# Normalising expert outputs group by group inside the expert stage, with the scatter-adds of a step no longer waiting for one another

## The chip, the cores and the metric

One core of one Trainium2 chip runs the whole program. The metric is device time in microseconds, the median of three runs. The engines are TensorE (PE in the rows; PEld is its weight load), VectorE (DVE), ScalarE (ACT), GpSimd (POOL) and SyncE (SP), whose queue issues plain transfers; GpSimd issues the indirect ones (gather and scatter by a list of row numbers).

## What is computed

One layer over 4096 tokens of width 1024, in float32: a Fourier mixer, a layer norm, a mixture of experts, and a second layer norm.

```
y = fourier_mixer(x, w_in, w_out)
x = layer_norm(ALPHA * x + y, ln_g[0], ln_b[0])
scores = sigmoid(x @ w_router)                 # 32 experts in 4 groups of 8
group = argmax(sum of the two best (scores + b_router) of each group)
expert_idx = the two best experts inside that group
y = sum over the two experts of gate * (silu(x @ w_gate[e]) * (x @ w_up[e])) @ w_down[e]
x = layer_norm(ALPHA * x + y, ln_g[1], ln_b[1])
```

Both experts of a token lie in one group, so a token's sum is complete once the eight experts of its group are done. With the reference's inputs its routing gives the four groups 992, 1017, 1033 and 1054 tokens, and the experts, in order: 243, 248, 228, 257, 289, 307, 203, 209, 278, 289, 220, 242, 258, 266, 246, 235, 249, 265, 273, 272, 298, 202, 199, 308, 251, 239, 206, 278, 281, 245, 257 and 351.

## The kernel before

The first part (the Fourier mixer, the first norm and the router, in `GROUPS` = 16 steps) stores each normalised row twice: in `hd` ("h_rows"), from which the experts read, and in `acc` ("sums"), to which they add. GpSimd's `list_tokens` scatters (token, gate) entries into one list per expert. The lists are first filled with padding entries that point to spare rows behind the 4096 tokens.

The expert stage runs over *units* of up to `UNIT` = 320 tokens of one expert. A table `utab` gives a unit's expert and its row in the lists. An expert with at most 320 tokens is one unit; the last has two, so there are 33. A unit with at most `NARROW` = 256 tokens is *narrow* (17 of them), the others *wide* (16); a wide unit has a third, half-size token tile "c" beside "a" and "b". Each engine runs its own loop over units, tied to the others by semaphores:

- SyncE loads a unit's twelve weight pieces (`wraw`, six slots) and the entries of a coming unit (`load_entries`).
- ScalarE and VectorE split each piece in a high and a low part (`split`: cast on ScalarE, subtraction on VectorE), since each product is made of three passes.
- TensorE does the gate products (four blocks `k`), the up products (four blocks `k`, two PSUM banks, so that block 2 waits until VectorE has read block 0), the transposes of the next unit's rows, and then the down products.
- VectorE multiplies gate and up (`hid`), ScalarE casts it (`hidT` high part), VectorE makes the low part. The down product needs all four.
- GpSimd scatter-adds the results `yrow_a`, `yrow_b` (and `yrow_c`) to `acc` and gathers rows for the unit after next (`xrow`).

In the unit of GpSimd the scatter-add of tile b waits for that of tile a to land. These lines are before's:

```
for t in range(2):
    ...
    if t:
        own_wait(pool, y_out, 32 * u + 16, pool_gate)
    scatter(t, P, y_out)
```

After the last unit a tail loads the 32 tiles of `acc` in row order, normalises each (VectorE statistics and gain, ScalarE root and scaling, GpSimd the addition of `ln_b`) and stores it.

## Time and profile before

| | |
|---|---|
| median of 3 runs | 2350.23 us (2346.81 to 2350.3) |
| profiled execution, its own time | 2350.37 us |
| its span in the trace | 2348.4 us |
| TensorE busy | 2127.3 us, 91% |
| VectorE, ScalarE, GpSimd busy | 58%, 43%, 25% |
| first part, until the first unit's matmuls | 0 to 860.6 us |
| units | 860.6 to about 2211 us |
| tail, after the last scatter-add has landed | 2219.0 to 2348.4 us |

An engine's busy share is an average over these three parts, so what a change is worth is read in the part where it acts. Times in rows are microseconds from the span's start unless marked ns.

### The profile page before, as it was taken

The page shows a single profiled execution, that of the slowest core. Times are in us where ns is not written, and L with a number is a line of the kernel's source. Part 1 is how long each engine was busy: PE and PEld are TensorE (multiplying, and loading weights), DVE is VectorE, ACT ScalarE, POOL GpSimd, SP SyncE. Part 2 cuts the span into 40 slices and gives each one's busy share as a digit, 9 for nine tenths or more (in the row PEclk, how much of TensorE's full clock was granted, in tenths as well). Part 3 has the DMA queues.
Part 4 walks back from the last instruction along what each step waited for, and adds up shares of the span by engine and source line. Part 5 has one row for each costly group of instructions (what it writes and reads, how often), then busy time and mean ns, then how long its engine had stood idle before and what let it go on. Part 6 is the DMA issues. An engine that isn't in the chain of part 4 may idle for free.

```text
span 2348.4 us, 37687 instructions
## 1 busy us (share of the span) xinstructions
PE 2127.3 (91%) x12222; PEld 1801.6 (77%) x12223; DVE 1373.1 (58%) x2254; ACT 998.2 (43%) x1442; POOL 582.7 (25%) x493
## 2 busy tenths in 40 slices
PE   8999899999999449999999999999999999999600
PEld 3443678888888349999999999999999999998500
DVE  3321148888887746555655656555555565555298
ACT  1221123333233226555555645655455565554143
POOL 1000034444544411211121121212111121211166
PEclk9999999999999769999999999999999999999855
DMA  6880233443333347767776866877677777766376
GB/s 226 283 287 21 67 126 113 147 147 125 116 127 108 126 153 210 222 203 195 219 216 184 248 194 211 227 223 197 180 220 218 219 218 228 209 202 183 98 286 238
DMA packets 136067, 435.59 MB, mean 185 GB/s; under 512 B 30912, under 2 KB 35008, under 8 KB 131904
## 3 DMA queue, kind: packets, MB, share of 16 engines
q1 hardware_dynamic: 98592, 307.12, 38.6%
q0 software_dynamic: 37440, 128.01, 21.6%
q8 instruction: 21, 0.34, 0.1%
q14 instruction: 14, 0.11, 0.0%
HBM read 328.01 MB, written 108.10 MB: 186 GB/s over the span
## 4 chain that ended last, share of the span: by engine, by line
PE 90%; POOL 3%; issue 3%; DMA 2%; DVE 2%; ACT 0%; SPq 0%; POOLq 0%; ACTq 0%; DVEq 0%
PE ps L877 36%; PE ps L901 15%; PE ps L759 15%; PE ps L696 5%; POOL fin_r L1689 3%; PE ps L865 3%; PE ps L741 3%; PE ps L909 2%; PE ps L715 2%; PE ps L793 2%; PE ps L650 1%; PE ps L780 1%; PE ps L700 1%; PE ps L870 1%; PE ps L659 1%
## 5 line engine op out<-in xcount | busy, mean ns | idle before, releaser
L901 PE MATMUL ps<-wd_hi,hidT 128*128 128x512 f32 x1056 | 293.0, 402 | 0.4 <-ACT hidT L1099 0.4
L1359 DVE TENSOR_TENSOR wd_lo<-wraw,wd_hi 128x1024 fp32r<-128x1024 f32 x132 | 161.9, 1226 | 199.0 <-ACT wd_hi L1057 198.7
L901 PEld LDWEIGHTS ps<-wd_hi,hidT 128*128 128x128 f32 x1056 | 190.1, 189 | 36.3 <-ACT hidT L1099 0.8
L1359 DVE TENSOR_TENSOR wg_lo<-wraw,wg_hi 128x1024 fp32r<-128x1024 f32 x132 | 161.4, 1224 | 92.6 <-ACT wg_hi L1057 92.5
L1632 POOL DMA_INDIRECT sums<-yrow_a,ent_now x33 | 57.2, 1733 | 558.4 <-DVE yrow_a L1422 515.4
L1359 DVE TENSOR_TENSOR wu_lo<-wraw,wu_hi 128x1024 fp32r<-128x1024 f32 x132 | 160.7, 1218 | 52.0 <-ACT wu_hi L1057 51.9
L877 PE MATMUL ps<-mxT_hi,wg_hi 128*128 128x256 f32 (+1 forms) x1056 | 163.3, 297 | 13.4 <-issue 13.4
L1099 ACT CAST hidT<-hid 128x320 fp32r<-128x320 f32 x132 | 60.7, 460 | 257.3 <-DVE hid L1440 257.3
L877 PEld LDWEIGHTS ps<-mxT_hi,wg_hi 128*128 128x128 f32 x1056 | 149.7, 191 | 17.9 <-issue 16.0
L877 PE MATMUL ps<-mxT_lo,wg_hi 128*128 128x256 f32 (+1 forms) x1056 | 163.2, 297 | 0.0
L877 PE MATMUL ps<-mxT_hi,wg_lo 128*128 128x256 f32 (+1 forms) x1056 | 162.6, 297 | 0.0
L877 PE MATMUL ps<-mxT_hi,wu_lo 128*128 128x256 f32 (+1 forms) x1056 | 162.0, 296 | 0.0
L877 PE MATMUL ps<-mxT_hi,wu_hi 128*128 128x256 f32 (+1 forms) x1056 | 161.8, 296 | 0.0
L877 PE MATMUL ps<-mxT_lo,wu_hi 128*128 128x256 f32 (+1 forms) x1056 | 161.8, 296 | 0.0
L1057 ACT CAST wu_hi<-wraw 128x1024 fp32r<-128x1024 f32 x132 | 135.8, 1054 | 36.6 <-DMA wraw<-expert_w_up 31.8
L877 PEld LDWEIGHTS ps<-mxT_lo,wg_hi 128*128 128x128 f32 x1056 | 149.3, 192 | 0.0
L877 PEld LDWEIGHTS ps<-mxT_hi,wg_lo 128*128 128x128 f32 x1056 | 148.7, 191 | 0.0
L877 PEld LDWEIGHTS ps<-mxT_lo,wu_hi 128*128 128x128 f32 x1056 | 147.9, 190 | 0.0
L877 PEld LDWEIGHTS ps<-mxT_hi,wu_hi 128*128 128x128 f32 x1056 | 147.9, 190 | 0.0
L877 PEld LDWEIGHTS ps<-mxT_hi,wu_lo 128*128 128x128 f32 x1056 | 147.9, 190 | 0.0
L1005 ACT CAST xt_hi<-ps 128x256 fp32r<-128x256 f32 x128 | 41.4, 375 | 246.9 <-PE ps L741 246.9
L901 PE MATMUL ps<-wd_lo,hidT 128*128 128x512 f32 x528 | 142.3, 391 | 0.0
(212 smaller groups left out, 4120.0 us busy)
## 6 DMA issues: line engine op xcount, KB each, us to landing
wraw<-expert_w_gate SPq DMA_DIRECT2D x132, 512.0 KB, 5.4
wraw<-expert_w_up SPq DMA_DIRECT2D x132, 512.0 KB, 5.4
wraw<-expert_w_down SPq DMA_DIRECT2D x132, 512.0 KB, 4.4
xch<-x SPq DMA_DIRECT2D x16, 1024.0 KB, 6.7
first_stage<-ych SPq DMA_DIRECT2D x16, 1024.0 KB, 8.3
yt<-first_stage SPq DMA_DIRECT2D x16, 1024.0 KB, 4.9
fin_r<-sums SPq DMA_DIRECT2D x32, 512.0 KB, 3.9
out<-fin_r SPq DMA_DIRECT2D x32, 512.0 KB, 2.9
```

The source lines that it names most:

```text
L696: mm = nc.tensor.matmul(dst, foldT[:, m, g, c * P:(c + 1) * P], T[:, m, g, h * HALF:(h + 1) * HALF], start=(g == 0), stop=(m == 1 and g == ...
L715: nc.tensor.matmul(bank[s1_bank(n)], f1, xch[:, b, n % 4 // 2, n % 2 * HALF:(n % 2 + 1) * HALF], start=True, stop=True).then_inc(job_ps, 1)
L741: mm = nc.tensor.matmul(s2_bank(jj)[:, lo:lo + P], yt[:, b, q, cc * P:(cc + 1) * P], m2t[:, b, q, :], start=True, stop=True)
L759: mm = nc.tensor.matmul(ps[:, cols], xt[l][:, m, c, :], w[r][:, c, cols], start=(n == 0 and c == 0 and not edge_row), stop=(n == 2 and c = ...
L865: mm = nc.tensor.transpose(psT[k % 2][:, lo:lo + P], xrow_s[t][:, c, :], ident)
L877: mm = nc.tensor.matmul(ps[k % 2][:, 0:n], w[l][:, c, k * P:(k + 1) * P], mxT[r][:, c, 0:n], start=(i == c == 0), stop=(i == 2 and c == CH ...
L901: mm = nc.tensor.matmul(psY[h], hidT[:, l, c, t * P:(t + 1) * P], wd[r][:, c, cols], start=(i == c == 0), stop=(i == 2 and c == FC - 1))
L1057: nc.scalar.copy(piece(0, j), wraw[:, j % SLOTS, :]).then_inc(whi_ok, 1)
L1099: nc.scalar.copy(hidT[:, 0, k, :], hid[:, k % 2, :]).then_inc(hh_ev, 1)
L1359: nc.vector.tensor_tensor(piece(1, j), wraw[:, j % SLOTS, :], piece(0, j).bitcast(F32), ALU.subtract).then_inc(wlo_ok, 1)
L1632: pool.indirect_dma_start(acc, bass.IndirectOffsetOnAxis(ap=ent_now[0:n, t, 0:1], axis=0), yrow[t], None, compute_op=ALU.add).then_inc(don ...
L1689: nc.gpsimd.tensor_tensor(fin_r[:, b, :], fin_r[:, b, :], lnb2, ALU.add).then_inc(fh_ok, 1)
```

## The change

The normalisation of a tile of 128 tokens moves from the tail into the units. The router writes, beside the 32 expert lists, four *group lists* (`LISTS` = 36), with the group's tokens. A table `ltab`, made once by `ln_table`, says for each unit which group tile it normalises: from the first unit behind a group's last expert on, one tile per unit. A unit that has none ready takes the first tile anyhow, whose rows are written again later. The tiles per group are 8, 8, 9 and 9 (34, the last of each overlapping the one before it); units 8 to 32 take 25, and the tail takes the rest in a batch of `FB` = 10, by gathers and scatters. All of this goes through one buffer, `lnrow`, one entry tile, `lent`, and one table slot per unit. In a unit, GpSimd gathers `lnrow` first, VectorE, ScalarE and VectorE work on it between their other work, and GpSimd stores it behind the scatter-add of tile a. The scatter-adds a and b no longer wait for one another; all are waited for at the unit's end, with the store. Padding entries point to 512 spare rows in place of 128, all different within one scatter; to fill them, and the longer lists, is more to write at the start.

```diff
-USED_ROWS = S // LANES + 2
+LISTS = E + EG
+CAP = 35 * P
+FILL = 512
-FB = 8
+FB = 10
...
# SyncE, first part
-            sp.dma_start(acc[S:S + P, :], x[0:P, :]).then_inc(pad_out, 16)
-            sp.dma_start(hd[S:S + P, :], x[0:P, :]).then_inc(pad_out, 16)
+            sp.dma_start(acc[S:S + FILL, :], x[0:FILL, :]).then_inc(pad_out, 16)
+            sp.dma_start(hd[S:S + FILL, :], x[0:FILL, :]).then_inc(pad_out, 16)
...
# SyncE, units: load_unit
                 for j in range(PIECES):
                     load_piece(u, e, j)
+                    if j == 9:
+                        tile = ln_slot(u)
+                        own_wait(sp, lrow_out, 16 * u, sp_gate)
+                        load_ln_tile(tile)
...
# ScalarE, unit
+            def ln_deviation(u):
+                act.wait_ge(lvar_ok, u + 1)
+                nc.scalar.activation(lnstd[:, 0:1], lnmv[:, 0, 1:2], ACT.Sqrt, bias=eps2_c).then_inc(lstd_ok, 1)
+            def ln_normal(u):
+                act.wait_ge(lsh_ok, u + 1)
+                nc.scalar.activation(lnrow, lnrow, ACT.Identity, bias=lnsh[:, 0:1], scale=lnrs[:, 0:1]
+                                     ).then_inc(lnorm_ok, 1)
...
                     nc.scalar.copy(hidT[:, 0, k, :], hid[:, k % 2, :]).then_inc(hh_ev, 1)
+                    if k == 0:
+                        ln_deviation(u)
+                    if k == 1:
+                        ln_normal(u)
...
# VectorE, unit
+            def ln_statistics(u):
+                dve.wait_ge(lrow_in, 16 * u + 16)
+                step.begin(unit_steps + LN_STEPS * u)
+                statistics(lnrow, 0).then_inc(lvar_ok, 1)
...
                 for k in range(FC):
                     split(u, GU_PIECES + k)
+                ln_statistics(u)
                 for k in range(FC):
                     if more and k < FC - 1:
                         split(u + 1, k)
+                    if k == 1:
+                        ln_invert(u)
+                    if k == 3:
+                        ln_gain(u)
...
                     turn_x(u + 1, 1)
+                ln_shift(u)
...
# GpSimd, list_tokens: 2 x 3 scatters in place of 2 x 2, and the unit
+            def ln_gather(u):
+                own_wait(pool, lent_in, 16 * u + 16, pool_gate)
+                pool.indirect_dma_start(lnrow, None, acc, bass.IndirectOffsetOnAxis(ap=lent[:, 0:1], axis=0)
+                                        ).then_inc(lrow_in, 16)
+            def ln_store(u):
+                own_wait(pool, lfin_ok, u + 1, pool_gate)
+                pool.indirect_dma_start(out, bass.IndirectOffsetOnAxis(ap=lent[:, 0:1], axis=0), lnrow, None
+                                        ).then_inc(lrow_out, 16)
             def unit(u, ahead):
                 wide = unit_wide(pool, u)
+                ln_gather(u)
                 for t in range(2):
                     pool.wait_ge(ya_ok, 2 * u + t + 3)
                     own_wait(pool, yd_ok, 2 * u + t + 3, pool_gate)
-                    if t:
-                        own_wait(pool, y_out, 32 * u + 16, pool_gate)
                     scatter(t, P, y_out)
+                    if t == 0:
+                        ln_store(u)
                 if ahead == 2:
                     turned(u + 1)
                     gather(u + 2)
                     gather_c(u + 2)
-                own_wait(pool, y_out, 32 * u + 32, pool_gate)
                 with pool.If(wide > 0):
                     ...
+                own_wait(pool, y_out, 32 * u + 32, pool_gate)
+                own_wait(pool, lrow_out, 16 * u + 16, pool_gate)
...
# GpSimd, tail
+            with pool.Fori(0, batches(pool)) as i:
+                own_wait(pool, lents_in, 16 * FB * i + 16 * FB, pool_gate)
+                for b in range(FB):
+                    pool.indirect_dma_start(fin_r[:, b, :], None, acc, ...).then_inc(fin_in[b], 16)
+                for b in range(FB):
+                    if b:
+                        own_wait(pool, fin_out, 16 * FB * i + 16 * b, pool_gate)
+                    own_wait(pool, fh_ok, FB * i + b + 1, pool_gate)
+                    pool.indirect_dma_start(out, ..., fin_r[:, b, :], None).then_inc(fin_out, 16)
```

On GpSimd, where the prelude ends and a unit begins, before (the first row is the last copy ahead of the loop, `y_out` counts landed scatter-adds):

```order
L1675 COPY ent_next<-ent_in 128x6 [waits xrow_in]
L461 TENSOR_LOAD utab [waits ent_ok]
L461 ISA x2
L1678 UNCONDITIONAL_BRANCH
L1678 ISA
L454 TENSOR_LOAD utab
L454 ISA x2
L1642 ISA
L1632 DMA sums<-yrow_a,ent_now 4224x1024 [waits ya_ok,yd_ok]
L1642 REGISTER_ALU
L120 ISA [waits ya_ok,yd_ok]
L1632 DMA sums<-yrow_b,ent_now 4224x1024 [waits y_out]
```

The same place in the changed kernel:

```order
L120 ISA
L1741 DMA lnrow<-sums,lent 128x1024 [waits lent_in]
L1753 ISA
L1732 DMA sums<-yrow_a,ent_now 4608x1024 [waits ya_ok,yd_ok]
L120 REGISTER_ALU
L1746 DMA out<-lnrow,lent 4096x1024 [waits lfin_ok]
L1753 REGISTER_ALU
L1732 DMA sums<-yrow_b,ent_now 4608x1024 [waits ya_ok,yd_ok]
```

The gather of `lnrow` is now a unit's first transfer, behind everything that the unit before it issued and waited for; the store stands between scatter-adds a and b, and b's wait on `y_out` is gone.

On VectorE, from the last `wd` splits of a unit to the first `hid` product, before:

```order
L1359 TENSOR_TENSOR wd_lo<-wraw,wd_hi 128x1024 [waits whi_ok]
L1358 ISA
L1359 TENSOR_TENSOR wg_lo<-wraw,wg_hi 128x1024 [waits whi_ok]
L1438 ISA
L1440 TENSOR_TENSOR hid<-sgate,ps 128x320 [waits silu_ok,u_ps]
```

And in the changed kernel:

```order
L1393 TENSOR_TENSOR wd_lo<-wraw,wd_hi 128x1024 [waits whi_ok]
L1512 ISA
L1249 BN_STATS lnst<-lnrow 128x6 [waits lrow_in]
L1250 BN_STATS lnst<-lnrow 128x6
L141 ISA
L1252 BN_AGGR lnmv<-lnst 128x2 [waits dve_step]
L1392 ISA
L1393 TENSOR_TENSOR wg_lo<-wraw,wg_hi 128x1024 [waits whi_ok]
L1542 ISA
L1544 TENSOR_TENSOR hid<-sgate,ps 128x320 [waits silu_ok,u_ps]
```

The statistics, with their wait on `lrow_in` (the gather of `lnrow`), now stand ahead of the first `hid` product of the unit.

## Rows read from the trace of the kernel before

**Rows 1.** The page, busy time, share and instructions of TensorE.

```profile
PE 2127.3 (91%) x12222; PEld 1801.6 (77%) x12223; DVE 1373.1 (58%) x2254; ACT 998.2 (43%) x1442; POOL 582.7 (25%) x493
```

**Rows 2.** The chain that ended last, over units: start us, us, what.

```profile
1506.36 23.04 PE ps L877 x192
...
1589.31 28.16 PE ps L877 x192
...
2170.34 3.27 issue
2173.62 24.79 PE ps L877 x192
```

**Rows 3.** Timeline of GpSimd around two units: start us, us, what, [idle before <-releaser].

```profile
1502.09 1.77 POOL L1632 DMA_INDIRECT sums<-yrow_a,ent_now  x1 [13.90 <-DVE yrow_a L1422]
1511.16 1.57 POOL L1632 DMA_INDIRECT sums<-yrow_b,ent_now  x1 [7.31 <-DMA sums<-yrow_a,ent_now]
...
1515.93 0.92 POOL L1621 DMA_INDIRECT xrow_c<-h_rows,ent_in  x1 [0.30 <-issue]
...
1525.30 0.19 POOL L1661 COPY ent_next<-ent_in 128x6 int32<-128x6 int32 x1 [4.71 <-DMA xrow_c<-h_rows,ent_in]
...
1606.66 0.19 POOL L1661 COPY ent_next<-ent_in 128x6 int32<-128x6 int32 x1 [1.74 <-issue]
```

**Rows 4.** Timeline of VectorE in the same two units.

```profile
1506.87 0.75 DVE L1422 TENSOR_SCALAR yrow_b<-ps,ent_now 128x512 f32<-128x512 f32 x1
...
1516.43 1.23 DVE L1359 TENSOR_TENSOR wd_lo<-wraw,wd_hi 128x1024 fp32r<-128x1024 f32 x1 [1.65 <-ACT wd_hi L1057]
...
1520.79 0.49 DVE L1440 TENSOR_TENSOR hid<-sgate,ps 128x320 f32<-128x320 f32 x1 [0.25 <-PE ps L877]
...
1606.94 0.49 DVE L1440 TENSOR_TENSOR hid<-sgate,ps 128x320 f32<-128x320 f32 x1 [0.89 <-PE ps L877]
```

**Rows 5.** Timeline of ScalarE in the same two units.

```profile
1506.94 1.28 ACT L1057 ACT_TABLE_LOAD   x1 [0.30 <-issue]
1508.23 1.05 ACT L1057 CAST wd_hi<-wraw 128x1024 fp32r<-128x1024 f32 x1
...
1529.95 0.46 ACT L1099 CAST hidT<-hid 128x320 fp32r<-128x320 f32 x1 [1.04 <-DVE hid L1440]
...
1618.03 0.46 ACT L1099 CAST hidT<-hid 128x320 fp32r<-128x320 f32 x1 [2.11 <-DVE hid L1440]
```

**Rows 6.** DMA issues: count, median us from issue to landing.

```profile
ent_in<-expert_lists SPq DMA_DIRECT2D x66, 1.0 KB, 2.0
...
xrow_a<-h_rows,ent_in POOLq DMA_INDIRECT x33, 8.0
...
rows<-x,rowg POOLq DMA_INDIRECT x32, 5.0
h_rows<-rows,rowg POOLq DMA_INDIRECT x32, 3.8
```

**Rows 7.** Groups of the tail: busy us, mean ns, idle before.

```profile
L1495 DVE TENSOR_TENSOR fin_r<-fin_r,lng 128x1024 f32<-128x1024 f32 x32 | 40.9, 1278 | 0.2 <-ACT fin_r L1144 0.2
L1144 ACT ACTIVATE fin_r<-fin_r,lnsh,lnrs 128x1024 f32<-128x1024 f32 x32 | 39.7, 1240 | 19.6 <-DVE lnsh L1484 19.6
...
L1215 DVE BATCH_NORM_STATS2 lnst<-fin_r 128x6 f32<-128x512 f32 x32 | 21.8, 681 | 15.0 <-DMA fin_r<-sums 15.0
...
L1139 ACT ACTIVATE lnstd<-lnmv,eps_c 128x1 f32<-128x1 f32 x32 | 9.4, 295 | 61.7 <-DVE lnmv L1218 61.7
```

**Rows 8.** The chain that ended last, from the last scatter-adds into the tail.

```profile
2213.01 5.97 DMA sums<-yrow_b,ent_now
...
2220.64 7.21 DMA lnb<-ln_b
```

**Rows 9.** A window of the start: us, busy per engine, clock, DMA share, GB/s.

```profile
40.00:60.00 20.00, 20.00 (x101) 10.49 (x100) 7.39 (x11) 6.26 (x11) 0.00 (x0) 1.00 0.00 0
```

**Rows 10.** Timeline of VectorE between router and first unit.

```profile
847.85 0.69 DVE L1403 TENSOR_TENSOR mxT_lo<-ps,mxT_hi 128x512 fp32r<-128x512 f32 x1 [6.41 <-ACT mxT_hi L1061]
```

More of the change, by code:

```diff
@@ L277, in trunk_kernel @@
         mid = keep.take("mid", CH * NG)
-        padl = keep.take("padl", 2 * USED_ROWS, I32)[0:LANES, :]
+        lent = keep.take("lent", 2, I32)
+        lents_t = keep.take("lents", 2 * FB, I32)
+        pad_at = keep.byte / 1024
+        padl = [keep.take(n, 2 * CAP // P, I32) for n in ("pad_e", "pad_g")]
+        keep.take("ltab_end", 8)
+        ltab = at("ltab", pad_at, LANES + LN_COLS + 2, I32)[0:1, :]
         def small(name, *dims):
@@ L852, in _ @@
             mm.then_inc(utab_ps, 1)
+            pe.wait_ge(lcol_made, 1)
+            for k in range(2):
+                mm = nc.tensor.matmul(psLtab[:, k * P:(k + 1) * P], lcol[:, k:k + 1], ident,
+                                      start=True, stop=True)
+            mm.then_inc(ltab_ps, 1)
             pe.sem_inc(y1_ps, 2)
@@ L1431, in unit, with ln_gain, ln_shift @@
+            def ln_gain(u):
+                dve.wait_ge(lnorm_ok, u + 1)
+                nc.vector.tensor_tensor(lnrow, lnrow, lng2, ALU.mult).then_inc(lgain_ok, 1)
+            def ln_shift(u):
+                dve.wait_ge(lgain_ok, u + 1)
+                nc.vector.tensor_tensor(lnrow, lnrow, lnb2, ALU.add).then_inc(lfin_ok, 1)
             def unit(u, more):
@@ L1471, in _ @@
                 split(0, j)
+            ln_table()
             for k in range(4):
@@ L1476, in _, with normal @@
             dve.sem_inc(yc_ok, 2)
+            dve.wait_ge(ln2_in, 32)
+            unit_steps = step.start + step.k
             all_units(dve, unit)
+            units = dve.value_load(utab[:, 4 * LANES:4 * LANES + 1], min_val=E, max_val=MAX_UNITS)
+            def normal(t, i, b):
+                dve.wait_ge(fin_in[b], 16 * i + 16)
+                step.begin(unit_steps + LN_STEPS * units + t)
+                statistics(fin_r[:, b, :], b % LB).then_inc(fn_ok, 1)
             def invert(t, b):
-                b %= LB
@@ L1507, in _ @@
-            start = step.start + step.k
-            for b in range(FB):
-                fin(b, 0, b)
-            with dve.Fori(1, TILES // FB) as i:
-                for b in range(FB):
-                    fin(FB * i + b, i, b)
-            step.begin(start + 2 * TILES - 1)
-            invert(TILES - 1, FB - 1)
-            gain(TILES - 2, FB - 2)
-            gain(TILES - 1, FB - 1)
+                nc.vector.tensor_tensor(fin_r[:, b, :], fin_r[:, b, :], lng2, ALU.mult).then_inc(fb_ok, 1)
@@ new lines, in gain @@
+                dve.wait_ge(fb_ok, t + 1)
+                nc.vector.tensor_tensor(fin_r[:, b, :], fin_r[:, b, :], lnb2, ALU.add).then_inc(fh_ok, 1)
+            with dve.Fori(0, batches(dve)) as i:
+                for b in range(FB + 2):
+                    if b < FB:
+                        normal(FB * i + b, i, b)
+                    if 0 < b <= FB:
+                        invert(FB * i + b - 1, (b - 1) % LB)
+                    if b >= 2:
+                        gain(FB * i + b - 2, b - 2)
```

280 lines of the change are left out of this document (162 added, 118 removed).

## Prediction

> **What bounds the kernel now.** I read the page first: TensorE is busy 91% of the span [rows 1]. The chain that ended last says where. Through the units it is TensorE without a gap: 192 gate and up matmuls take 23.04 us in a narrow unit and 28.16 in a wide one [rows 2]. So in the units nothing that VectorE, ScalarE or GpSimd does costs anything, as long as each result is there when TensorE asks. In the tail TensorE does nothing: the last scatter-add lands at 2213.01 + 5.97 = 2219.0 [rows 8], the span ends at 2348.4, and 129.4 us pass in normalising 32 tiles. The change trades that tail for work in the units, so the timelines of three engines must say whether the work fits there. I count each from t0, the unit's first matmul: 1506.36 for a narrow unit, 1589.31 for a wide one [rows 2].
>
> VectorE ends its last `wd` split at 1516.43 + 1.23, t0 + 11.3, and the first `hid` product at 1521.28, t0 + 14.9; in the wide unit the product ends at 1607.43, t0 + 18.1 [rows 4]. ScalarE ends the fourth `hidT` cast, for which the down products wait, at 1530.41, t0 + 24.05, and at 1618.49, t0 + 29.2, in the wide one [rows 5]. GpSimd lags: it still works off the unit before. Its last copy, behind which its next unit begins, ends at 1525.49, t0 + 19.1, and 1606.85, t0 + 17.5 [rows 3]. That lag is hidden today, because GpSimd's next task is a scatter-add needed only at the unit's end.
>
> **The gather comes too late.** In the change GpSimd's unit begins with the gather of `lnrow`, and VectorE waits for it ahead of the first `hid` product. Behind that wait are queued: a split, `hid`, and so TensorE's up block 2, then everything to the down products.
>
> When does GpSimd's unit begin? The removed wait lets scatter-add b go earlier. It was issued at 1511.16 though `yrow_b` was done at 1507.62 [rows 3, 4]; of these 3.5 us I give 2.7 back, since the release of a wait takes something too. If all behind it moves along, the unit begins at t0 + 16.5 after a narrow unit and, taking the same off 17.5, at t0 + 14.8 after a wide one. Bounds: no gain at all (19.1 and 17.5), if the queue, which now carries the store of `lnrow` ahead of b, lands things as late as before; and t0 + 12.2, if the c gather (issued 2.7 earlier than 1515.93) lands in the 5.0 us of the router part's gathers [rows 3, 6].
>
> How long does the gather take? It has 512 KB, like `xrow_a`: 8.0 us beside weights and other gathers, 5.0 for `rows<-x` with little beside it [rows 6]. It goes alone but among weight loads: I take 6.5, with 0.3 to start, and 5.0 and 8.0 as bounds. The Trainium skill, DMA: Bandwidth & Descriptors, section on the anatomy of a DMA of the gpsimd path, gives 2.0 us plus bytes over 436,000 per us. By it 512 KB land in 3.2 us, an estimate that would take 32 x 3.3 = 106 us off my sum. The trace does not agree: 5.0 is the shortest median of a gather of this size here [rows 6].
>
> From landing to the end of the first `hid` product VectorE needs two statistics (0.68 each) and their aggregate, 1.6; a split, 1.2; the product, 0.5: 3.3 us [rows 4, 7]. So that product ends at 16.5 + 6.8 + 3.3 = t0 + 26.6 after a narrow unit, t0 + 24.9 after a wide one, against 14.9 and 18.1 now.
>
> **The chain behind it gets longer too.** From the first `hid` to the fourth `hidT` cast pass 9.1 us in a narrow unit and 11.1 in a wide one now [rows 4, 5], TensorE's pace. With the change: cast 0.5, table load for the root 1.3, root 0.3, ScalarE split 1.05, VectorE split 1.2, reciprocal and shift 0.35, `hid` 0.5, together 5.2; then cast 0.5, the scaling 1.24, both splits 2.25, `hid` 0.5, together 4.5; then cast, low part, gain (1.28), `hid` and cast, 3.2. That is 12.9 us in place of 9.1 or 11.1 [rows 4, 5, 7]. The down products thus start late by (H + 12.9 - 24.05) in a narrow and (H + 12.9 - 29.2) in a wide unit, H being the end of the first `hid`: 15.5 or 13.8 us in a narrow one (behind a narrow or a wide one), 10.3 or 8.6 in a wide one. By the experts' counts, of the 32 units after the first there are 9 narrow behind narrow, 7 narrow behind wide, 7 wide behind narrow, 9 wide behind wide: 139.5 + 96.6 + 72.1 + 77.4 = **386 us**. The delay does not heal itself: GpSimd's lag is counted from t0, so each unit pays anew. The first unit gets its gather early and pays nothing.
>
> For the table load the row shows 1.28 us and a cast that starts 0.01 us behind its end [rows 5]. The Trainium skill, ScalarE: Activation LUTs, section What ACT_TABLE_LOAD costs, has 2.66 us for a switch, with a drain, and its section on table sets advises to batch calls by set, which speaks against a root in every unit. By it the sum would be about 1.4 x 32 = 44 us higher, an estimate; no drain shows in this trace.
>
> TensorE restarts slowly after idling: behind 3.27 us idle its 192 matmuls took 24.79 us, not 23.04 [rows 2]. The new stall is before up block 2, where the chain above (5.2 us from `hid` to `hid`, against 23.04 / 8 = 2.9 us a block) covers those 1.75 us. I add nothing; 56 us over 32 units if it isn't covered.
>
> **What is hidden.** VectorE's shift (1.28, as the gain [rows 7]) sits beside down products, as does the store. SyncE waits for the store before it loads pieces 10 and 11; the store lands some microseconds behind t0, and splits of those pieces delayed by a few us end before the gather lands, so the first wait covers the second. Without that cover this wait would be next; piece 10 is cast at about t0 + 6.5 today and would come at about t0 + 12, so some 5 us per unit, 160 us. The two more list scatters per router step sit on GpSimd, which waits for TensorE there: nothing. The fills at the start write some 3.3 MB more; from 40 to 60 us the DMA engines are at 0.00 [rows 9], which holds it: 0 to 10 us, I take 1. `ln_table`'s 30 small VectorE operations run where it idles 6.41 us [rows 10], with a trip to TensorE: I take 2, bound 10.
>
> **The tail.** Units 8 to 32 take 25 of 34 tiles, so 9 are left, one batch. Behind the last landing: ten entry loads, 7 us if I take 0.7 for the issue of each, and 2.0 to land [rows 6]; the first gather, 5.0; about 8 until the first tile is through VectorE. Then one tile per 4.6 us: VectorE needs 1.6 + 0.5 + 2 x 1.28 = 4.6, and a store which waits for the one before it takes 3.8 and, I take, 0.8 for the release and the next issue [rows 6, 7]. 9 x 4.6 + 4.7 = 46. Together 68 us for 129.4, where the 7.21 us load of `lnb` [rows 8] is gone also: **-61 us**.
>
> **Sum**, against the span of 2348.4: + 386 + 3 - 61 = 2676. The profiled execution took 2350.37, 2 us more than its span and as much as the median of 2350.23: **2678 us**.
>
> **Rivals.** (a) The gather is hidden. This needs it landed by t0 + 11.3, so GpSimd's unit begun by t0 + 5. Then only the longer chain counts, 16 x 3.8 + 16 x 1.8 = 90: 2350 + 90 + 3 - 61 = 2382. Against it: scatter-add b alone can't be issued before t0 + 2 and is waited for. 8%. (b) Faster: the gather is hidden and ScalarE's table load, root and scaling fit between the casts as well, since ScalarE idles 2.11 us before a wide unit's cast [rows 5]; then 2350 + 3 - 61 = 2292. It decides at the same t0 + 11.3, and needs a 2.9 us slot per narrow block to hold 5.2. 5%. (c) Worse: SyncE's wait for the store delays weights beyond the gather's landing, or gathers land slower than 8.0 in the fuller queue: above 2830. 8%. (d) A uniform small gain or no change, from causes above cancelling: 2%. The forecast gets 77%.
>
> **Range.** Low: unit begun at t0 + 12.2, gather 5.0, H = 20.8, 16 x 9.7 + 16 x 4.5 = 227: 2519. High: no gain from the removed wait, gather 8.0, H = 29.9 on average, 16 x 18.8 + 16 x 13.6 = 518: 2810, and 10 or more for the start. So 2510 to 2830. About 0.2%, 5 us, can be told from no change; faster 5%, same 1%, slower 94%.
>
> **What would show it.** In the chain of a unit: a wait of VectorE for DMA `lnrow<-sums` of 7 to 12 us ahead of the first statistics, and TensorE idle between up blocks 1 and 2. The matmul sum stays; a narrow unit takes about 14 to 15 us longer, a wide one 9 to 10. GpSimd's unit begins 15 to 17 us behind t0. The tail takes about 68 us with nine or ten stores 4.6 us apart. I am wrong if VectorE's wait for `lnrow` is under 3 us, if GpSimd's unit begins early, or if the weights' wait replaces it.

## The result

The changed kernel takes 2768.68 us (median of 4 runs, 2758.12 to 2774.82), the kernel before 2350.27 (4 runs, 2346.81 to 2351.41): ratio 1.1778, 95% interval [1.1739, 1.1818]. It is slower by 418 us, 91 more than predicted. The profiled execution took 2766.32 us, with a span of 2764.2.

The span splits at two points that every trace shows: the first matmul of the first unit, and the landing of the last scatter-add.

| stretch | before | after | difference | predicted |
|---|---|---|---|---|
| start to the first unit's first matmul | 860.6 | 866.4 | +5.8 | +3 |
| units, to the last landing | 1358.4 | 1819.9 | +461.5 | +386 |
| tail | 129.4 | 77.9 | -51.5 | -61 |

The page of the changed kernel: busy time, granted clock in 40 slices, the chain by engine and by line, and two groups (busy us, mean ns, idle time ahead and what ended it).

```profile
PE 2235.0 (81%) x12226; PEld 1876.5 (68%) x12227; DVE 1424.2 (52%) x2383; ACT 1055.9 (38%) x1497; POOL 617.1 (22%) x580
...
PEclk9999999999976888889988998999889988998985
...
PE 43%; DMA 22%; issue 14%; ACT 8%; DVE 8%; POOLq 3%; POOL 2%; SPq 0%; ACTq 0%; DVEq 0%
...
L897 PE MATMUL ps<-mxT_hi,wu_hi 128*128 128x256 f32 (+1 forms) x1056 | 196.8, 337 | 297.6 <-DVE hid L1544 297.5
...
L1249 DVE BATCH_NORM_STATS2 lnst<-lnrow 128x6 f32<-128x512 f32 x33 | 22.9, 694 | 315.5 <-DMA lnrow<-sums,lent 315.5
```

TensorE's busy share falls from 91% [rows 1] to 81%. It now idles 297.5 us in front of up blocks, for `hid`. VectorE idles 315.5 us in front of the first statistics, for the gather. No single engine replaces TensorE as the bound: 22% of the chain are transfers and 14% issue, and the chain goes round through GpSimd, a gather, VectorE, ScalarE and TensorE.

The waits of the changed kernel: us in total, times, longest.

```profile
DVE lnst L1249 <- DMA lnrow<-sums,lent: 315.5, 31, 14.3
...
PE ps L897 <- DVE hid L1544: 297.5, 37, 14.0
...
ACT wd_hi L1077 <- DMA wraw<-expert_w_down: 125.6, 41, 10.4
...
POOL ent_next L1773 <- DMA xrow_c<-h_rows,ent_in: 105.0, 12, 9.3
...
POOL lnrow L1741 <- issue: 61.2, 33, 2.3
```

GpSimd in a wide unit behind a narrow one, whose first matmul starts at t0 = 1527.8; the like stretch of before is in [rows 3].

```profile
1529.52 1.82 POOL L1732 DMA_INDIRECT sums<-yrow_b,ent_now  x1 [3.79 <-issue]
...
1534.20 0.93 POOL L1721 DMA_INDIRECT xrow_c<-h_rows,ent_in  x1 [0.30 <-issue]
...
1545.50 0.19 POOL L1773 COPY ent_next<-ent_in 128x6 int32<-128x6 int32 x1 [9.00 <-DMA xrow_c<-h_rows,ent_in]
1547.53 0.97 POOL L1741 DMA_INDIRECT lnrow<-sums,lent  x1 [1.85 <-issue]
```

The gather goes out at t0 + 19.7. VectorE and ScalarE behind it, in the same unit [before: rows 4, 5]:

```profile
1554.14 0.69 DVE L1249 BATCH_NORM_STATS2 lnst<-lnrow 128x6 f32<-128x512 f32 x1 [11.10 <-DMA lnrow<-sums,lent]
...
1556.86 0.48 DVE L1544 TENSOR_TENSOR hid<-sgate,ps 128x320 f32<-128x320 f32 x1
...
1561.91 0.49 DVE L1544 TENSOR_TENSOR hid<-sgate,ps 128x320 f32<-128x320 f32 x1
```

```profile
1557.85 1.28 ACT L1103 ACT_TABLE_LOAD   x1
...
1562.43 0.46 ACT L1128 CAST hidT<-hid 128x320 fp32r<-128x320 f32 x1 [2.05 <-DVE hid L1544]
1562.79 1.24 ACT L1107 ACTIVATE lnrow<-lnrow,lnsh,lnrs 128x1024 f32<-128x1024 f32 x1
...
1569.21 0.46 ACT L1128 CAST hidT<-hid 128x320 fp32r<-128x320 f32 x1 [1.14 <-DVE hid L1544]
```

VectorE sits 11.10 us in front of the statistics. The first product ends at 1557.34, t0 + 29.6, the fourth cast at 1569.67, 12.3 us behind it. That is the mechanism of the prediction, with a later gather than it had.

### The profile page after: what moved, and what is told of

Its sections match the earlier page's. It is cut to its first block, busy times and chain, and to the rows that moved or that the text cites. A ratio compares the mean times of both kernels' runs of the same rounds, so it can differ in the third digit from the quotient of the medians.

```text
span 2764.2 us, 38374 instructions
## 1 busy us (share of the span) xinstructions
PE 2235.0 (81%) x12226; PEld 1876.5 (68%) x12227; DVE 1424.2 (52%) x2383; ACT 1055.9 (38%) x1497; POOL 617.1 (22%) x580
## 4 chain that ended last, share of the span: by engine, by line
PE 43%; DMA 22%; issue 14%; ACT 8%; DVE 8%; POOLq 3%; POOL 2%; SPq 0%; ACTq 0%; DVEq 0%
PE ps L774 13%; PE ps L921 11%; DMA lnrow<-sums,lent 8%; DMA sums<-yrow_c,ent_now 6%; DMA xrow_c<-h_rows,ent_in 5%; PE ps L711 4%; DVE hid L1544 2%; ACT wg_hi L1077 2%; ACT hidT L1128 2%; PE ps L756 2%; PE ps L730 2%; PE ps L808 2%; DMA xrow_b<-h_rows,ent_in 2%; PE ps L897 2%; ACT L1103 1%
## 5 line engine op out<-in xcount | busy, mean ns | idle before, releaser
L897 PE MATMUL ps<-mxT_hi,wu_hi 128*128 128x256 f32 (+1 forms) x1056 | 196.8, 337 | 297.6 <-DVE hid L1544 297.5
L897 PEld LDWEIGHTS ps<-mxT_hi,wu_hi 128*128 128x128 f32 x1056 | 173.6, 222 | 307.6 <-DVE hid L1544 307.1
L921 PE MATMUL ps<-wd_hi,hidT 128*128 128x512 f32 x1056 | 318.4, 421 | 60.1 <-ACT hidT L1128 60.0
L921 PEld LDWEIGHTS ps<-wd_hi,hidT 128*128 128x128 f32 x1056 | 199.1, 197 | 115.4 <-ACT hidT L1128 79.1
L1128 ACT CAST hidT<-hid 128x320 fp32r<-128x320 f32 x132 | 60.5, 458 | 534.2 <-DVE hid L1544 534.2
L1077 ACT CAST wd_hi<-wraw 128x1024 fp32r<-128x1024 f32 x132 | 137.9, 1045 | 126.4 <-DMA wraw<-expert_w_down 125.6
L1249 DVE BATCH_NORM_STATS2 lnst<-lnrow 128x6 f32<-128x512 f32 x33 | 22.9, 694 | 315.5 <-DMA lnrow<-sums,lent 315.5
L897 PE MATMUL ps<-mxT_lo,wu_hi 128*128 128x256 f32 (+1 forms) x1056 | 184.9, 324 | 0.0
L897 PEld LDWEIGHTS ps<-mxT_lo,wu_hi 128*128 128x128 f32 x1056 | 172.1, 219 | 0.0
L897 PE MATMUL ps<-mxT_hi,wu_lo 128*128 128x256 f32 (+1 forms) x1056 | 168.9, 304 | 0.0
L897 PEld LDWEIGHTS ps<-mxT_hi,wg_hi 128*128 128x128 f32 x1056 | 151.0, 193 | 20.1 <-issue 18.2
L897 PEld LDWEIGHTS ps<-mxT_hi,wu_lo 128*128 128x128 f32 x1056 | 156.8, 201 | 0.0
```

The lines of the kernel that those rows point to most:

```text
L897: mm = nc.tensor.matmul(ps[k % 2][:, 0:n], w[l][:, c, k * P:(k + 1) * P], mxT[r][:, c, 0:n], start=(i == c == 0), stop=(i == 2 and c == CH ...
L921: mm = nc.tensor.matmul(psY[h], hidT[:, l, c, t * P:(t + 1) * P], wd[r][:, c, cols], start=(i == c == 0), stop=(i == 2 and c == FC - 1))
L1077: nc.scalar.copy(piece(0, j), wraw[:, j % SLOTS, :]).then_inc(whi_ok, 1)
L1128: nc.scalar.copy(hidT[:, 0, k, :], hid[:, k % 2, :]).then_inc(hh_ev, 1)
```

## The experiments

All times are compared with the kernel before on the same chip. I use two measures: the median time, and the length of the units in the trace, from the first unit's first matmul to the issue of the last scatter-add b. The second is needed because of an offset in the routing stage that some runs have (last section). It is 1352.4 us before (860.61 to 2213.01) and 1814.2 after (866.37 to 2680.55). The length of the units comes from one execution of each kernel, and the last column of the table compares runs of several chips. The profiled execution lies within 4 us of the median in all kernels but two: e_wait_back's took 2816.9 for a median of 2801.3, e_compute's 2379.7 for 2386.4. The four executions of after lie up to 16.7 us apart.

| kernel | median us | ratio, 95% interval | units us | against after |
|---|---|---|---|---|
| before | 2350 | | 1352.4 | -461.8 |
| after | 2768.7 | 1.1778 [1.1739, 1.1818] | 1814.2 | |
| e_nothing | 2301.6 | 0.9797 [0.9780, 0.9813] | 1351.4 | -462.8 |
| e_compute | 2386.4 | 1.0167 [1.0141, 1.0194] | 1430.3 | -383.9 |
| e_transfers | 2360.3 | 1.0045 [1.0028, 1.0061] | 1408.3 | -405.9 |
| e_tr_early | 2325.5 | 0.9886 [0.9870, 0.9902] | 1353.3 | -460.9 |
| e_notable | 2705.4 | 1.1508 [1.1483, 1.1534] | 1753.7 | -60.5 |
| e_spfree | 2778.1 | 1.1815 [1.1796, 1.1835] | 1808.3 | -5.9 |
| e_wait_back | 2801.3 | 1.1898 [1.1874, 1.1922] | 1843.6 | +29.4 |
| e_gather_first | 2567.8 | 1.0919 [1.0901, 1.0937] | 1619.3 | -194.9 |
| v2_end | 2351.9 | 0.9996 [0.9984, 1.0008] | 1381.7 | -432.5 |
| v2_again | 2355.9 | 1.0015 [1.0005, 1.0025] | 1381.2 | -433.0 |
| v5_order | 2324.3 | 0.9888 [0.9872, 0.9905] | 1371.4 | -442.8 |
| v6_finfirst | 2348.0 | 0.9984 [0.9973, 0.9995] | 1372.9 | -441.3 |

**Theory:** the units are longer because VectorE waits for a late gather in front of the first `hid` product. **Rivals:** the arithmetic costs it, wherever it stands; the transfers do; or SyncE's wait for the store makes the weights late.

### e_nothing, e_compute, e_transfers: the parts apart

```diff
# e_nothing: no entry load, gather, arithmetic or store in a unit
-                ln_gather(u)
-                ln_statistics(u)
-                        ln_store(u)
...
# e_compute: as the change, but on a constant tile, without gather, store, entry load
-                dve.wait_ge(lrow_in, 16 * u + 16)
+                dve.wait_ge(lfin_ok, u + 1)
+            link(nc.vector.memset(lnrow, 1.0))
...
# e_transfers: no arithmetic; GpSimd waits for the gather ahead of scatter-add a
-                own_wait(pool, lfin_ok, u + 1, pool_gate)
+                own_wait(pool, lrow_in, 16 * u + 16, pool_gate)
```

> The changed kernel with the normalisation left out of the units (no gather, no arithmetic, no store there); the tail still normalises its last ten tiles, so most of the output is not made. What is left are the lists and tables, the two scatter-adds without a wait between them, and the short tail. Theory (the units' loss comes from what stands in them for the normalisation): the first part later by 5.8 us and the tail shorter by 51.5 us, as the two traces have them, so 2350 + 5.8 - 51.5 = about 2305 us. Rival (the scatter-adds without a wait, or the longer lists, cost something in every unit): clearly above 2350.

> The arithmetic of the normalisation stays in its places in the units (statistics, root, scaling, gain, shift), on a tile that is set to ones once; the gather, the store and the entry loads of the units are left out, so the output is not made. Theory (VectorE's wait for the gather is most of the loss): only the longer chain behind the first product is left. By the changed kernel's trace it is 12.3 us against 9.1 and 11.1 before, so 16 x 3.2 + 16 x 1.2 = 70 us over the kernel without any of it, about 2375 us. Rival (the arithmetic and the table load are the loss, and the wait only fills what would be idle anyway): above 2600 us.

> The gather and the store of a tile stay in each unit, with SyncE's wait for the store, but no arithmetic and so no wait of VectorE for the gather: GpSimd itself waits for it ahead of the next scatter-add, and what is stored is not normalised. Theory: the transfers are off TensorE's path, about 2305 to 2330 us. Rival (traffic or SyncE's wait for the store makes weights late, and that is the loss or would take its place): 2400 us or more, with ScalarE's splits of the wd pieces waiting for DMA in the chain.

Without any of it the units last 1351.4 us, as before (1352.4). So the missing wait between scatter-adds and the longer lists neither help nor hurt there, and the shorter tail, less the 5.4 us of the longer start, is worth 2350 - 2302 = 49 us. The arithmetic in its places, with nothing to wait for, costs 79 us in the units (70 expected); by its median it is some 7 us more. The transfers alone cost 57; their 2360 us lie between the two expectations, 30 above the theory's and 40 below the rival's. Together that is 136, and the change costs 463: **327 us arise only when the arithmetic must wait for the gather**. The sum still counts SyncE's wait, which the gather covers in the change (next section). With that wait taken out of all the kernels, the two halves cost 81 us apart and 457 together.

The 57 us of e_transfers come from SyncE. Its queue in that kernel, around one unit (issue rows):

```profile
1012.37 8.46 SPq L598 DMA_DIRECT2D wraw<-expert_w_down  x2
1033.31 0.34 SPq L589 DMA_DIRECT2D lent<-token_lists  x1
1034.04 1.02 SPq L598 DMA_DIRECT2D wraw<-expert_w_down  x2
```

The `lent` load waits until 1033.31 for the store to land, and the last two `wd` pieces stand behind it. ScalarE then waits for them:

```profile
ACT wd_hi L1077 <- DMA wraw<-expert_w_down: 118.9, 43, 9.0
```

### e_tr_early and e_spfree: SyncE without its wait

```diff
# both: GpSimd copies the entries, gathers and stores by the copy
+                nc.gpsimd.tensor_copy(lentn, lent).then_inc(lcopy_ok, 1)
# SyncE waits for the copy alone
-                        own_wait(sp, lrow_out, 16 * u, sp_gate)
+                        own_wait(sp, lcopy_ok, u, sp_gate)
```

> As e_transfers (gather, wait for it in front of scatter-add a, store of the rows without any arithmetic, so that the output isn't normalised), but with the copied address list, so that SyncE's load waits for the copy and no longer for the store. Theory (of e_transfers' 59 us over the kernel without both, most came from weights that were late behind SyncE's wait, 4.6 to 5.1% of its chain): 2305 to 2325 us. Rival (the transfers cost by what they take from the DMA engines or from GpSimd): 2345 to 2360 us.

> The changed kernel with one edit: GpSimd copies the 128 list entries of the tile to a second place and gathers and stores by the copy, so that SyncE's load of the next entries waits for the copy alone and no longer for the store to land. Theory (the gather sets the unit's length, SyncE's wait is covered): 2750 to 2775 us. Rival (part of the 75 us by which the units cost more than 386 comes of weights that are late behind SyncE's wait): 59 us or more less, 2710 or below.

With the copy, the transfers alone cost 1.9 us in the units in place of 57 (1353.3 against 1351.4); ScalarE's wait for `wraw<-expert_w_down` is gone from its list of waits. The median of 2325.5, at the edge of the expected 2305 to 2325, hides this: that run's first unit starts at 886.88, 21 us late. SyncE in e_tr_early, the same two issues:

```profile
1022.58 8.46 SPq L598 DMA_DIRECT2D wraw<-expert_w_down  x2
1032.66 0.34 SPq L589 DMA_DIRECT2D lent<-token_lists  x1
```

In the changed kernel the same edit takes only 5.9 us off the units, which is within the spread of after's executions. ScalarE's 125.6 us of waiting for `wraw<-expert_w_down` are gone, and VectorE waits that much sooner, and longer, for the gather, 404.9 us for 315.5:

```profile
DVE lnst L1249 <- DMA lnrow<-sums,lentn: 404.9, 31, 16.6
```

So SyncE's wait is real and has its price where nothing covers it, and is covered by the gather's wait in the change, as predicted. By its median e_spfree is 9 us slower than after, 3 above its expectation; its first unit starts at 883.05, 16.7 us later than after's.

### e_notable: the table load

> The changed kernel with the root in the units replaced by an addition of the same shape that needs no table load (the normalised values are wrong by it); the rest stays. Theory (the load sits in the chain from the first product to the down products, 1.28 us in each unit that waits): about 42 us less than the changed kernel, 2727 us. If a switch of tables cost 2.66 us: about 85 us less, 2684 us. If the load were hidden: no difference from 2769 us.

```diff
-nc.scalar.activation(lnstd[:, 0:1], lnmv[:, 0, 1:2], ACT.Sqrt, bias=eps2_c)
+nc.scalar.activation(lnstd[:, 0:1], lnmv[:, 0, 1:2], ACT.Identity, bias=eps2_c)
```

The variance stands in place of its root, so the scale is another one. The units lose 60.5 us, 1.8 per unit, for a load of 1.28, and the median of 2705 lies between the expected 2727 and 2684. From the first `hid` to the fourth cast pass 10.92 us instead of 12.33 (means over the narrow units behind narrow ones): the load and 0.1. Over the 31 units between the first and the last these are 43 us; another 18 are gained between the fourth cast and the next unit's first matmul, and 6 are lost ahead of the first `hid`. The 18 come with TensorE's clock: in that stretch the granted clock is 1.00 in all 31 units of e_notable, and 0.87 to 0.90 in 12 of after's. The Trainium skill, ScalarE: Activation LUTs, section What ACT_TABLE_LOAD costs, gives 2.66 us for each switch with a drain: 88 us over 33 units, an estimate. The run lies between it and 42, and inside the chain it is little more than the row's 1.28 that counts.

### e_wait_back: the removed wait

```diff
                 for t in range(2):
+                    if t:
+                        own_wait(pool, y_out, 32 * u + 16, pool_gate)
                     scatter(t, P, y_out)
```

> The changed kernel with the wait between scatter-adds a and b put back, as before the change. The kernel without the normalisation in its units gained nothing that it could have from the removal (2301.6 against 2305 worked out with none). Theory: what stands behind scatter b on GpSimd moves back some microseconds per unit where the store is issued between the two, so the time rises by 0 to 3 us per unit, 2769 to 2860 us. Rival (scatter-adds that overlap slow each other and the gather): the time falls by 1 us per unit or more, 2735 or below.

The units take 29.4 us longer, but the profiled execution is the longest of its four, 15.7 us above their median; median against median, each less the start of its first unit, leaves 11 us. So the second half of the change is worth 0.3 to 0.9 us per unit here, and the lower figure isn't clear of the spread. The gather is issued 1.2 us later in narrow units behind narrow ones, 0.1 in wide ones behind wide ones (means, counted from the unit's first `sgate`). The sign is the theory's; the prediction had taken 2.7 in all.

### e_gather_first: the same work, the gather earlier

```diff
                 wide = unit_wide(pool, u)
-                ln_gather(u)
...
                 own_wait(pool, lrow_out, 16 * u + 16, pool_gate)
                 if ahead:
+                    ln_gather(u + 1)
                     nc.gpsimd.tensor_copy(ent_now, ent_next).then_inc(entc_ok, 1)
```

> The changed kernel with e_spfree's copied address list (2778 us by itself), and one order changed: GpSimd issues the gather of the next tile as soon as the scatter-adds and the store have landed, ahead of its copies of the entries and of the wait for the next unit's rows, instead of behind them. The arithmetic and its places stay. Theory (the landing of the gather sets when VectorE passes its statistics, and so the unit's length; it is issued 3 to 5 us per unit earlier, the wait for the rows being 105 us of 12 units and the issue gaps some 2 us): 2620 to 2700 us. Rival (the unit is set by the serial chain of arithmetic between VectorE and ScalarE, not by when the gather lands): 2760 us or more.

The deciding run. Nothing of the arithmetic moves, and the units lose 194.9 us (189 against e_spfree, its base). The median of 2567.8 is 52 below the theory's range. GpSimd and VectorE in a unit of it:

```profile
1562.99 0.18 POOL L1741 COPY lentn<-lent 128x2 int32<-128x2 int32 x1 [9.59 <-DMA sums<-yrow_c,ent_now]
1563.96 0.99 POOL L1743 DMA_INDIRECT lnrow<-sums,lentn  x1 [0.79 <-POOL lentn L1741]
1564.95 0.20 POOL L1771 COPY ent_now<-ent_next 128x6 int32<-128x6 int32 x1
```

```profile
1568.21 0.69 DVE L1249 BATCH_NORM_STATS2 lnst<-lnrow 128x6 f32<-128x512 f32 x1 [7.18 <-DMA lnrow<-sums,lentn]
```

From the issue of the gather to the first statistics pass 4.25 us, against 6.61 (1547.53 to 1554.14) in the changed kernel. So the edit pays twice: the gather goes out 5.7 us earlier in narrow units behind narrow ones (means from the first `sgate`: 9.5 for 15.2), 4.5 on the mean of all, and it lands faster, in 4.9 us for 6.8 on the mean of the 31 waits. In neither case is a transfer of GpSimd's own outstanding: `xrow_c` has been waited for. But in the changed kernel the copy that releases the gather releases SyncE's queue as well, and two weight loads start 0.3 and 0.9 us behind it (the third of the row below starts at 1556.97, when the gather has landed); in e_gather_first they come only after the gather. In the one unit of the changed kernel that waits for its gather with no weight load behind it, the last but one, it takes 4.26 us too. SyncE in the changed kernel, and the window of the gather in the changed kernel and in e_gather_first (the last three: granted clock, DMA share, GB/s):

```profile
1547.85 9.46 SPq L598 DMA_DIRECT2D wraw<-expert_w_up  x3
```

```profile
1547.50:1554.10 6.60, 1.56 (x11) 1.30 (x9) 0.00 (x0) 0.00 (x0) 0.97 (x1) 0.81 0.73 230
```

```profile
1564.00:1568.20 4.20, 3.00 (x26) 2.80 (x24) 0.00 (x0) 0.00 (x0) 1.33 (x3) 1.00 0.46 125
```

VectorE's wait for the gather falls from e_spfree's 404.9 us by 199, about what the units lose:

```profile
DVE lnst L1249 <- DMA lnrow<-sums,lentn: 205.7, 31, 10.6
```

### v2_end, v2_again, v5_order, v6_finfirst: off the path

```diff
# VectorE: statistics behind y_half(u, 0); at the unit's end, in place of ScalarE's scaling:
+                link(nc.vector.reciprocal(lnrs[:, 0:1], lnstd[:, 0:1]))
+                link(nc.vector.scalar_tensor_tensor(lnrow, lnrow, lnmv[:, 0, 0:1], lng2, ALU.subtract, ALU.mult))
+                nc.vector.scalar_tensor_tensor(lnrow, lnrow, lnrs[:, 0:1], lnb2, ALU.mult, ALU.add)
# GpSimd: the entries copied as in e_spfree, and a wait for the gather ahead of scatter-add a
# v2_end: the store behind the wait for scatter-add c
+                ln_store(u)
                 own_wait(pool, y_out, 32 * u + 32, pool_gate)
# v5_order: the store ahead of that wait, and its own wait behind the copies of the entries
```

> The same 33 tiles are normalised in the units, but off the path: VectorE takes the statistics of the gathered tile behind its first addition of a down product (the gather has had some 25 us by then), ScalarE the root behind the addresses of the next unit's short rows, and VectorE alone the gain, scale and shift at the unit's end (two operations of the kind (x - a) * b in place of ScalarE's scale and VectorE's gain and shift); GpSimd issues the store last in the unit, and copies the list of addresses, so that SyncE's next load doesn't wait for the store. Theory (what the change costs is VectorE's and ScalarE's wait for the gather, in front of the hid products): the units go back to about their length without the normalisation, and the time is 2305 to 2330 us, faster than before (2350) and after (2769). Rival (the price is the arithmetic and the transfers themselves, in whatever place): 2302 + 85 + 59 = 2446 us or more.

> v2_end with two edits on GpSimd alone: the store is issued behind scatter-add c instead of behind the wait for it, and the wait for the store stands behind the copies of the entries (in v2_end SyncE's loads of the next entries wait for those copies, and the last weight pieces stand behind them in SyncE's queue: its chain has 3.6% on the store and 1.7% on the late weights). Theory (that queueing is what v2_end has over e_tr_early's 2325): 2315 to 2335 us, faster than before by 0.6 to 1.5%. Rival (VectorE's and ScalarE's arithmetic at the unit's end keeps TensorE waiting for the evacuations): 2345 to 2355 us, no gain.

> v2_end once more, unchanged. In its trace, as in those of e_spfree, e_wait_back and e_tr_early, the first unit's matmuls start at 883 to 888 us; in every other kernel's, v5_order's with the same code ahead of the units among them, at 864 to 866 us: the routing stage was 2.7 us per group of tokens longer there. Theory (that offset belongs to those runs, not to the kernels, so stages must be compared, from the first unit's start to the last scatter-add): about 2330 us here, 20 less. Rival (it belongs to the kernel): 2352 us again.

> v5_order with one edit: VectorE's reciprocal, gain and shift stand in front of the two evacuations of a wide unit's short rows instead of behind them. Theory (the evacuations of the short rows give nothing to TensorE at once, and the store is issued 2 us earlier): 2315 to 2325 us. Rival (scatter-add c is issued later, and with it everything that GpSimd waits for at the unit's end): 2330 us or more.

With the same 33 tiles normalised, the units fall from 1814.2 to 1381.7 us in v2_end. Its median of 2351.9 is above the 2305 to 2330 expected, and 94 below the rival's 2446. What was left in it shows on GpSimd and SyncE:

```profile
1187.36 1.34 POOL L1748 DMA_INDIRECT out<-lnrow,lentn  x1 [0.30 <-issue]
1196.46 0.84 POOL L1771 COPY ent_now<-ent_next 128x6 int32<-128x6 int32 x1 [7.76 <-DMA out<-lnrow,lentn]
```

```profile
1199.48 0.39 SPq L581 DMA_DIRECT2D ent_in<-token_lists  x1
...
1201.40 2.28 SPq L598 DMA_DIRECT2D wraw<-expert_w_up  x4
```

```profile
1205.88 1.05 ACT L1077 CAST wu_hi<-wraw 128x1024 fp32r<-128x1024 f32 x1 [4.01 <-DMA wraw<-expert_w_up]
```

The store holds up GpSimd's copies, these SyncE's entry loads, these the `wu` pieces in its queue, and ScalarE waits 4.01 us for one. In v5_order the copy no longer waits for the store:

```profile
1201.36 0.99 POOL L1748 DMA_INDIRECT out<-lnrow,lentn  x1 [0.30 <-issue]
1202.51 0.19 POOL L1771 COPY ent_now<-ent_next 128x6 int32<-128x6 int32 x1 [0.17 <-DMA sums<-yrow_b,ent_now]
```

That takes 10.3 us off the units, not the 17 to 37 that its expectation had: its median of 2324.3 is where I expected it, but the larger part of the step from 2352 is the routing offset, which v2_end's run has and v5_order's has not. Of the 1371.4 us, 18 are still more than with the transfers alone (e_tr_early). What v5_order has more than that kernel is one table load per unit and the arithmetic between the evacuations, and its store stands elsewhere; which of them costs it is not shown. Moving VectorE's part ahead of the short rows' evacuations (v6_finfirst) changed nothing, 1372.9.

v5_order is 1.1% faster than the kernel before on its chip, 0.9888 [0.9872, 0.9905], and so faster than the changed kernel too. v6_finfirst, with units of the same length, reached only 0.9984 [0.9973, 0.9995] on another, with the routing offset, and missed its 2315 to 2325; v2_again shows the same 2352 to 2356 as v2_end, and my expectation of 2330 for it was wrong.

## Why the prediction was right, and where it was off

**The direction, the mechanism and the place are as predicted.** VectorE waits 11.10 us for the gather in the unit shown and 10.2 on the mean of its 31 waits (the longest 14.3), where 7 to 12 were to be seen; TensorE stalls in front of up blocks for `hid`; and e_gather_first and e_compute separate cause from company. Rivals (a) and (b), a hidden gather, did not come true: it would have had to be issued by t0 + 5, and goes out at t0 + 19.7.

**Mis-sized: the term of the units, 386 for 461.5.** The delays of the 31 units between the first and the last, counted from each unit's first matmul in the timelines of both kernels, give its three parts. The predicted ones are for the same 31. (The first unit, taken as free, costs 5.5 us more.)

| part of the units' delay | predicted | measured |
|---|---|---|
| first `hid` later | 286 | 377 |
| chain to the fourth cast longer | 86 | 68 |
| behind the fourth cast | 0 | 12 |

The step that failed is "the unit begins at t0 + 16.5 after a narrow unit ... t0 + 14.8 after a wide one". Means of the changed kernel, us behind the unit's first matmul (the prediction's t0, from the chain, is some 0.2 us later than that matmul's row):

| unit | GpSimd's last copy ends | gather issued | begin as predicted | first `hid` ends, for |
|---|---|---|---|---|
| narrow behind narrow | 17.8 | 19.7 | 16.5 | 29.9, 26.6 |
| wide behind narrow | 17.5 | 19.4 | 16.5 | 29.2, 26.6 |
| wide behind wide | 16.5 | 18.3 | 14.8 | 28.1, 24.9 |
| narrow behind wide | 16.4 | 18.2 | 14.8 | 28.4, 24.9 |

The gather goes out 2.9 to 3.5 us late in each. I had let the unit begin where the copy ends, but 1.85 us of GpSimd's own issue stand between that copy and the gather (61.2 us in 33). And I had moved the copy forward by 2.7 us, with scatter-add b. That scatter-add does go out 2.6 to 2.7 us earlier behind a narrow unit (means: t0 + 2.3 for 5.0, 1.8 for 4.4), but the copy ends only 1.0 to 1.5 us earlier than before's. By e_wait_back the removed wait gives the gather 1.2 us at most. The upper bounds, t0 + 19.1 behind a narrow unit and 17.5 behind a wide one, were the better values, and even they are passed by 0.3 to 0.8 us. `xrow_c` lands 10.98 us behind its issue in the chain of the unit shown. That the total still lies inside the range is partly luck: the first `hid` ends at t0 + 28.9 on the mean, near the 29.9 of the upper bound, which had added the latest begin and the slowest gather, 8.0 us; a late begin alone took most of that room. For the same reason the units grew by more than the 14 to 15 us (narrow) and 9 to 10 (wide) that were to be seen: by 17.0 to 18.2 and 11.6 to 12.4.

**The gather itself was right.** It was taken with 6.8 us from begin to VectorE's release and took 6.6; from its issue to the end of the first `hid` pass 9.7 to 10.2 against 10.1. The Trainium skill's formula (DMA: Bandwidth & Descriptors), 3.2 us for these bytes, is met by no gather: the shortest of this size in any trace took 4.0 us (`rows<-x` in v2_again). The tail's indirect stores of the same bytes come near it, 3.3 us.

**The chain:** 12.33 us on the mean (narrow and wide alike) for 12.9.

**TensorE's slower clock was covered inside the stall, partly not behind it.** TensorE around the stall of the unit shown (start us, us of 8 matmuls), and the row of the window behind the stall (its last three: granted clock, DMA share, GB/s):

```profile
1547.73 1.34 PE L897 MATMUL ps<-mxT_hi,wu_lo 128*128 128x320 f32 x8
1557.40 2.50 PE L897 MATMUL ps<-mxT_hi,wu_hi 128*128 128x320 f32 x8 [8.33 <-DVE hid L1544]
1559.70 2.33 PE L897 MATMUL ps<-mxT_lo,wu_hi 128*128 128x320 f32 x8
1561.83 1.36 PE L897 MATMUL ps<-mxT_hi,wu_lo 128*128 128x320 f32 x8
```

```profile
1557.00:1570.00 13.00, 11.18 (x60) 10.71 (x61) 7.22 (x13) 7.71 (x11) 0.00 (x0) 0.81 0.37 121
```

Behind 8.33 us idle the first 16 matmuls take 2.50 and 2.33 us per 8, where 1.34 is the full pace: that is TensorE at its lower level of 1.2 GHz and not at 2.4, and over the window the granted clock is 0.81. The 2.2 us lost are covered: the product that needs this up block starts only at 1566.14, and TensorE has ended the block at 1563.19.

Behind the fourth cast it is not covered in every unit. The stretch from that cast to the next unit's first matmul, in two neighbouring narrow units, each followed by a narrow one:

```profile
2235.21:2246.60 11.39, 11.34 (x54) 9.46 (x54) 8.79 (x12) 7.11 (x11) 2.78 (x2) 1.00 0.30 63
2288.08:2301.03 12.95, 12.90 (x54) 10.60 (x55) 8.98 (x12) 7.24 (x11) 2.81 (x2) 0.87 0.28 59
```

The same number of matmuls takes 1.56 us longer at a granted clock of 0.87. In 12 of the 31 units the clock is 0.87 to 0.90 there and the stretch is 1.2 to 1.5 us longer than before's, 16 us in all; in the others it is 1.00 and the stretch in nearly all 0.2 us shorter. That is a second fall of the clock, not the one behind the gather's stall: it is also in e_compute, which has no gather to wait for, in 9 of 31 units. In the slower of the two units above TensorE first waits 2.05 us for the last cast:

```profile
2288.13 0.50 PE L921 MATMUL ps<-wd_hi,hidT 128*128 128x512 f32 x1 [2.05 <-ACT hidT L1128]
```

So the restart that I had weighed costs nothing in the unit shown, as taken, and 16 us are lost to one that I hadn't seen: more than the whole of the table's last row.

**SyncE's wait** was covered, as said: 5.9 us or less when it is taken out (e_spfree). Rival (c) is off the table for the change, but it was a true cost: 55 us (1408.3 against 1353.3) where the gather didn't cover it. The 5 us per unit, 160 in all, that I gave it uncovered were three times too much.

**The start** costs 5.8 us in place of 3, inside its bounds.

**The tail** was taken for 10 us too little. Its chain, then GpSimd's first gather and its first, second and last stores, and VectorE's first statistics:

```profile
2680.55 5.74 DMA sums<-yrow_b,ent_now
2698.47 1.69 DMA lents<-token_lists
```

```profile
2701.01 0.99 POOL L1800 DMA_INDIRECT fin_r<-sums,lents  x1 [18.88 <-DMA lents<-token_lists]
...
2714.98 0.98 POOL L1807 DMA_INDIRECT out<-fin_r,lents  x1 [1.30 <-DVE fin_r L1605]
2721.12 0.98 POOL L1807 DMA_INDIRECT out<-fin_r,lents  x1 [5.16 <-DMA out<-fin_r,lents]
...
2757.41 0.95 POOL L1807 DMA_INDIRECT out<-fin_r,lents  x1 [3.31 <-DMA out<-fin_r,lents]
```

```profile
2705.48 0.69 DVE L1249 BATCH_NORM_STATS2 lnst<-fin_r 128x6 f32<-128x512 f32 x1 [25.70 <-DMA fin_r<-sums,lents]
```

From the last landing (2686.29) to the first gather pass 14.7 us, not 9: the ten entry loads and what surrounds them. The gather took 4.5 (5.0 taken), and the first tile is through VectorE and issued 9.5 us behind it (8 taken). The ten stores then go out 42.4 / 9 = 4.7 us apart on the mean, as I had it (4.6, nine times), and 6.8 us pass from the last issue to the end (4.7 taken).

## What to carry to other kernels

Before you move work into a stage bound by another engine, find the point at which its input can arrive, counted from the stage's start, and put the consumer behind it: the same gather and the same arithmetic cost 462 us in front of the `hid` products and 267 with the gather issued 4.5 us earlier on the mean; behind them, with the scaling on VectorE, 19 to 29. A software pipeline's queue engine may lag by half a stage without any cost (19.1 of 37 us here), and the lag becomes the price as soon as something needed early is put at its end: count from the row of its last instruction, and add its own issue time to the next. Take out each half by itself as well, since here the two halves cost 136 us apart and 463 together.

## What the runs showed of the hardware that I had not expected

**The same gather of 512 KB takes 4.25 or 6.61 us** until it releases VectorE, with the DMA engines at 0.46 or at 0.73 meanwhile (means over the kernels' 31 waits: 4.9 and 6.8). What releases it also decides what it must share the engines with. No run moved the weight loads alone.

**TensorE's clock fell in the down products too, and only with the long chain ahead of them.** The granted clock of that stretch is below 1.00 in 12 of 31 units of the changed kernel, 9 of e_compute and 16 of e_gather_first. It is 1.00 in all 31 of before, e_nothing, e_transfers and e_tr_early, and of e_notable, which has the arithmetic in its places but one table load less. TensorE's waits for `hidT` at that point come to 60.0 us in the changed kernel and 27.7 in e_notable. Why some units keep the full clock behind such a wait isn't shown.

**The routing stage has an offset of about 20 us in some runs.** The first unit's first matmul starts at 864 to 867 us in after, e_nothing, e_compute (863.5), e_transfers, e_notable, e_gather_first and v5_order, and at 883 to 891 in e_tr_early, e_spfree, e_wait_back, v2_end, v2_again and v6_finfirst. The edits don't explain the split: v5_order and v6_finfirst differ in one place within the units, and v2_end has it twice. The six that have it ran on two chips, the other experiments on two others; that the chip is the cause isn't shown. In the routing stage GpSimd waits longer for the list positions (v2_end, then v5_order; us, times, longest, from 100 to 880 us):

```profile
POOL token_lists L1655 <- DVE desti L1347: 115.3, 15, 11.3
```

```profile
POOL token_lists L1655 <- DVE desti L1347: 79.2, 15, 7.9
```

The kernel before, which scatters to two lists per token and not three, shows no such step in its medians (2350.2 to 2352.3 on the four chips). What makes the difference stays open. Whether v5_order would beat the kernel before where the offset stands was not run; v6_finfirst, with equal units, was 4 us faster there, not 27.
